# One inference step of a hybrid decoder: the first of seven products completed in PSUM, ScalarE's copies ahead of its roundings, the second weight sum on VectorE

## The reference

```python
def macaron_ffn(x, g_pre, w_gate, w_up, w_down, g_post):      # FFN_DIM = 4096
    n = rms_norm(x, g_pre)
    f = (jax.nn.silu(n @ w_gate) * (n @ w_up)) @ w_down
    return x + 0.5 * rms_norm(f, g_post)

h = macaron_ffn(x, ffn1...)      # stage one
h = token_mixing(h, ...)         # spatial gating and a causal depthwise convolution
h = cross_attend(h, ...)         # 4 heads over 256 memory tokens
h = macaron_ffn(h, ffn2...)      # stage two
```

## Time and profile before

| | before |
|---|---|
| time, median of 3 runs | 1690.36 us (1689.71 to 1690.53) |
| profiled execution, time / span | 1686.61 / 1684.7 us |
| TensorE matmul busy | 1580.3 us, 94% of the span |
| VectorE busy | 1321.5 us, 78% |
| ScalarE busy | 840.4 us, 50% |
| GpSimd busy | 425.3 us, 25% |
| mean granted TensorE clock | 0.994 |

### The profile page before, as it was taken

One profiled execution on the slowest core, in us unless ns is written; L12 is line 12 of the kernel. 1 busy time (PEld: TensorE's weight loads), 2 busy tenths in 40 slices (PEclk: granted clock), 3 DMA queues, 4 the chain that ended last, 5 costly groups with the idle time before them and its releaser, 6 DMA issues.

```text
span 1684.7 us, 28941 instructions
## 1 busy us (share of the span) xinstructions
PE 1580.3 (94%) x11628; PEld 1504.7 (89%) x11628; DVE 1321.5 (78%) x1715; ACT 840.4 (50%) x1496; POOL 425.3 (25%) x319
## 2 busy tenths in 40 slices
PE   8999999999999979999999999989999999999987
PEld 7998999999899969998989869889999998999987
DVE  5878888888888886999454533888888888888886
ACT  6455555554555555652453433555554545455444
POOL 2022433424243330000010100012334242433424
PEclk9999999999999989999999999999999999999998
DMA  5132223232222332233353543123232323223221
GB/s 172 51 101 89 87 76 100 76 101 76 91 86 76 101 118 67 76 101 114 101 177 110 194 146 101 35 72 96 78 99 75 101 76 97 79 78 99 76 76 57
DMA packets 121460, 159.12 MB, mean 94 GB/s; under 512 B 3645, under 2 KB 98449, under 8 KB 121320
## 3 DMA queue, kind: packets, MB, share of 16 engines
q1 hardware_dynamic: 115744, 138.16, 25.9%
q0 software_dynamic: 5488, 19.10, 3.3%
q10 hardware_dynamic: 96, 0.02, 0.0%
HBM read 152.22 MB, written 5.40 MB: 94 GB/s over the span
## 4 chain that ended last, share of the span: by engine, by line
PE 45%; DVE 36%; issue 10%; ACT 5%; POOL 2%; DMA 1%; DVEq 0%; SPq 0%; ACTq 0%; POOLq 0%
PE slot L2370 22%; PE slot L2169 15%; DVE mo L1548 5%; DVE wu L1646 4%; DVE f L1956 4%; DVE q L1637 4%; POOL raw L737 2%; DVE wu L1641 2%; PE slot L2215 2%; DVE wu L1656 2%; DVE turned L1552 1%; DVE wu L1651 1%; ACT wu L992 1%; DVE f L1758 1%; DVE wu L1661 1%
## 5 line engine op out<-in xcount | busy, mean ns | idle before, releaser
L2370 PE MATMUL slot<-nb,wu 128*128 128x288 f32 x4704 | 653.8, 297 | 58.2 <-ACT part L1046 25.4
L2370 PEld LDWEIGHTS slot<-nb,wu 128*128 128x128 f32 x4704 | 630.4, 188 | 77.9 <-ACT part L1046 34.8
L2370 PE MATMUL slot<-mo,wu 128*128 128x288 f32 x2688 | 373.1, 297 | 13.1 <-DVE mo L1548 3.8
L2370 PEld LDWEIGHTS slot<-mo,wu 128*128 128x128 f32 x2688 | 360.6, 188 | 23.0 <-issue 8.9
L737 POOL TENSOR_TENSOR raw<-raw,q 128x512 f32<-128x512 f32 x88 | 118.9, 1351 | 729.2 <-DVE q L1637 555.5
L1656 DVE TENSOR_TENSOR wu<-raw,wu 128x1024 fp32r<-128x1024 f32 x88 | 141.1, 1603 | 34.4 <-ACT wu L992 34.4
L742 POOL TENSOR_TENSOR raw<-raw 128x512 f32<-128x512 f32 x88 | 118.3, 1344 | 132.6 <-DVE wu L1651 132.6
L1646 DVE TENSOR_TENSOR wu<-q,wu 128x1024 fp32r<-128x1024 f32 x86 | 130.9, 1522 | 19.8 <-ACT wu L985 19.8
L1034 ACT ACTIVATE part<-slot 128x288 f32<-128x288 f32 (+1 forms) x84 | 41.3, 491 | 204.8 <-PE slot L2370 204.8
L2169 PE MATMUL slot<-mid,wp 128*128 128x288 f32 x960 | 133.0, 297 | 4.4 <-DVE mid L1480 2.3
L2169 PE MATMUL slot<-n,wp 128*128 128x288 f32 x960 | 134.8, 298 | 2.1 <-issue 1.7
(11 more groups left out here) (305 smaller groups left out, 2130.2 us busy)
## 6 DMA issues: line engine op xcount, KB each, us to landing
raw<-in_ffn_w_gate_dram SPq DMA_DIRECT2D x32, 1024.0 KB, 5.3
raw<-in_ffn_w_up_dram SPq DMA_DIRECT2D x32, 1024.0 KB, 5.4
raw<-in_ffn_w_down_dram SPq DMA_DIRECT2D x64, 512.0 KB, 4.3
raw<-in_mix_w_in_dram SPq DMA_DIRECT2D x8, 1024.0 KB, 5.5
kring<-in_cache_mem_k_dram POOLq DMA_DIRECT2D x6, 1024.0 KB, 5.2
raw<-in_xattn_w_k_dram SPq DMA_DIRECT2D x4, 1024.0 KB, 5.0
raw<-in_xattn_w_v_dram SPq DMA_DIRECT2D x4, 1024.0 KB, 5.0
raw<-in_mix_w_out_dram SPq DMA_DIRECT2D x4, 1024.0 KB, 5.0
```

The costliest lines, as they stand in the source:

```text
L2370: ins = pe.matmul(dst[:, q, 0:HALF], wu[:, p, wi, unit], x[:, xi], start=begins, stop=bool(ends), skip_group_check=not (start and 0 in pairs))
```

## The change

- **P1 completed in PSUM.** `copy_p1` copies x not to `part1` but to the y place, and P2 is added there. `take_c11` goes: in a gate group ScalarE takes its Silu straight from y (`silu_c11`), in an up group `multiply_c11` multiplies y by the gate. `take_y` adds y to f at once, `add_p1` on GpSimd goes, and `part1` with it.
- **`sum_q4` on VectorE** in place of GpSimd, behind take_c22 and its multiplication.
- **ScalarE's order.** copy_p7 and high_q13 come ahead of the roundings of 2 and 4; in a down group copy_p1(n+1) comes behind high_a2(n+1).
- **VectorE's order.** conv_low 756 right behind late_sum; take_c22 right behind low_q2; low_q13 ahead of conv_low 2 and 4; take_x ahead of low_a2; multiply_c21 ahead of low_a2; conv_low 3 and 1 behind early_sums.
- **Head.** low_a2, high_a2, copy_p1 of group 0 ahead of the second pair's sums and roundings.
- **End.** The operands 5, 6 and 7 of the last pair are summed and rounded one by one; the last group's P6 and P7 parts are added by VectorE straight from PSUM (`take_second`, `take_third`); its P3 comes ahead of P4; fewer rows are added on VectorE and more on TensorE (`ROW_SUMS`); memory_roots comes behind the root of stage one and memory_rows behind pre2's.

The diff, cut to its core (places, counts and renamed semaphores of the parts above are left out):

```diff
@@ GpSimd, ffn @@
-                def sum_q4(n): ...
-                def add_p1(n):
-                    pool.wait_ge(p1_copied, group_count(name, n))
-                    nc.gpsimd.tensor_tensor(f_part(n, 0, 1), f_part(n, 0, 1), part1[:, :, :], ALU.add).then_inc(f11_part, 1)
-                    if adds(n):
+                    if adds(n) and n + 1 < NG:
                         add_p6(n)
-                    if n + 1 < NG:
-                        sum_q4(n + 1)
-                    if adds(n):
+                    if adds(n) and n + 1 < NG:
                         subtract_p7(n)
-                    if adds(n + 1):
-                        add_p1(n + 1)
@@ ScalarE, ffn @@
                 def copy_p1(n):
+                    u = group_use(name, n, "y")
                     act.wait_ge(p1_done, group_count(name, n))
-                        dst = part_of(n, part1, 0)
-                    nc.scalar.activation(dst, x_of(n), ACT.Copy).then_inc(p1_copied, 1)
+                    act.wait_ge(slot_free[u % 4], u // 4)
+                    before = GATES_BEFORE[n]["y"]
+                    if before is not None:
+                        act.wait_ge(c21_silu, gated_count(name, pair_of(before)))
+                    nc.scalar.activation(y_of(n), x_of(n), ACT.Copy).then_inc(p1_copied, 1)
+                def silu_c11(n):
+                    ...
+                    act.wait_ge(p2_done, group_count(name, n))
+                    free(nc.scalar.activation(gate_c[:, 0, t1], y_of(n), ACT.Silu), group_use(name, n, "y"))
                 def silu_rest(n):
-                    nc.scalar.activation(gate_c[:, 0], gate_c[:, 0], ACT.Silu).then_inc(c11_silu, 1)
+                    nc.scalar.activation(gate_c[:, 0, t2], gate_c[:, 0, t2], ACT.Silu).then_inc(c12_silu, 1)
+                def last_up(n):
+                    conv_high("5", LAST_PAIR, (s75_sum, turned_count(name, LAST_PAIR)))
+                    conv_high("6", LAST_PAIR, (s6_sum, pair_count(name, LAST_PAIR)))
+                    act.wait_ge(job_done, group_jobs(name, n))
+                    high_q4(n + 1)
+                    copy_p1(n + 1)
+                    conv_high("2", LAST_PAIR, (c12_mul, gated_count(name, LAST_PAIR)))
+                    high_a11(n + 2)
@@ first_group @@
+                    high_a2(0)
+                    copy_p1(0)
                     conv_high("1", 1, made_plain(1, 1))
-                    copy_p1(0)
-                    conv_sums_of(1)
-                    high_a2(0)
-                    conv_high("4", 1, (s4_sum, pair_count(name, 1)))
                     high_a11(1)
                     high_q4(0)
+                    conv_sums_of(1)
@@ group @@
                     copy_p6(n)
+                    if n == LAST_UP + 1:
+                        conv_high("7", ...)
+                        conv_high("4", ...)
                     if is_kind(n - 1, "gate"):
                         silu_rest(n - 1)
-                            conv_sums(n - 1)
-                            conv_late(n - 1)
+                    if turn:
+                        conv_sums(n - 1)
                     if more:
                         high_q2(n + 1)
+                    if is_kind(n, "gate"):
+                        silu_c11(n)
                     copy_p7(n)
                     if more:
                         high_q13(n + 1)
-                        if n != LAST_UP:
+                        if n != LAST_UP and not is_kind(n, "down"):
                             copy_p1(n + 1)
+                    if turn:
+                        conv_late(n - 1)
                     if is_kind(n, "up"):
                         conv_early(n)
                     if more:
                         high_a2(n + 1)
+                        if is_kind(n, "down"):
+                            copy_p1(n + 1)
@@ VectorE, ffn @@
+                def sum_q4(n):
+                    s = group_slab(name, n)
+                    dve.wait_ge(q2_lo, group_count(name, n))
+                    V.tensor_tensor(a11_of(s), a12_of(s), a11_of(s), ALU.add).then_inc(q4_sum, 1)
-                def take_c11(n): ...
                 def multiply_c11(n):
-                    V.tensor_tensor(up_c[:, 0, t1], up_c[:, 0, t1], gate_c[:, 0, t1], ALU.mult).then_inc(c11_mul, 1)
+                    dve.wait_ge(*y_freed(name, n - 1))
+                    dve.wait_ge(p2_done, group_count(name, n))
+                    u = group_use(name, n, "y")
+                    free(V.tensor_tensor(up_c[:, 0, t1], slot(u)[:, 0, 0:HALF], gate_c[:, 0, t1], ALU.mult), u)
@@ group: the whole new order @@
                     if n == LAST_UP + 1:
                         for k in ("7", "4", "3"): conv_low(k, LAST_PAIR)
                     if n == 0:
                         sum_4(1); take_c22(0)
                     elif more:
                         sum_q13(n + 1)
                     if turn:
                         late_sum(n - 1); conv_low("756", pair_of(n - 1))
                     if adds(n): take_p5(n)
                     if down: take_y(n)
                     if up: multiply_c11(n)
                     if more: low_q2(n + 1)
                     if down and not adds(n): take_p5(n)
                     elif n and not down: take_c22(n)
                     if up: multiply_c22(n)
                     if more:
                         sum_q4(n + 1); low_q13(n + 1)
                     if turn:
                         conv_low("2", pair_of(n - 1)); conv_low("4", pair_of(n - 1))
                     if n == LAST_UP: conv_low("1", pair_of(n))
                     if up: multiply_c21(n)
                     if down: take_x(n)
                     if more and n != LAST_UP: low_a2(n + 1)
                     if up: early_sums(n)
                     if n == LAST_UP:
                         take_c12(n); multiply_c12(n); low_a2(n + 1); conv_low("2", LAST_PAIR)
                         sum_7(LAST_PAIR); sum_4(LAST_PAIR); low_a11(n + 2)
                     else:
                         if up:
                             for k in ("3", "1"): conv_low(k, pair_of(n))
                         if n + 2 < NG: low_a11(n + 2)
                         if down: take_z(n)
                         else: take_c12(n)
                     if more: low_q4(n + 1)
@@ last_group @@
                     take_p5(n)
+                    take_second(n)
                     take_y(n)
+                    take_third(n)
                     add_rows(slice(0, T), 2, 1, 0)
-                    if beside:
-                        beside()
-                    for i in (4, 6):
+                    for i in (4, 6) if not behind else ():
                         add_rows(t2, 5, i)
+                    take_z(n)
+                    for i in (5, 7) if not behind else ():
+                        add_rows(slice(0, 2 * P), 6, i)
                     take_x(n)
-                    for i in (5, 7):
-                        add_rows(t1, 6, i)
-                    take_z(n)
-                    for i in (5, 7):
-                        add_rows(t2, 7, i)
@@ TensorE @@
                 def p2(n):
-                    wait_place(n, "y")
+                    pe.wait_ge(p1_copied, count(n))
-                    product(n, P2, y_of(n), True, [p2_done])
+                    product(n, P2, y_of(n), False, [p2_done])
@@ last_groups @@
-                    group(d + 1)
+                    p6(d + 1)
+                    p2(d + 1)
+                    p7(d + 1)
+                    p3(d + 1, False)
+                    p4(d + 1, True)
@@ sum_rest @@
-                pe.wait_ge(f_added, 9 * (STAGE["ffn1"] + 1))
+                pe.wait_ge(f_added, rows_added("ffn1"))
                 fold_in(name, facc, True, True)
-                for i in (4, 6):
-                    for j in range(2):
+                for tiles, strips, count in (((4, 6), (2, 3), 5), ((5, 7), (0, 1), 6), ((4, 6), (0, 1), 7), ((5, 7), (2, 3), 8)):
+                    pe.wait_ge(f_squared, 8 * STAGE["ffn1"] + count)
+                    for i in tiles:
+                        for j in strips:
```

More of the change, by code:

```diff
@@ L757, in ffn @@
                 sum_q2(0)
-                sum_q4(0)
                 for n in range(NG):
@@ L1189, in ffn, with others @@
                 if name == "ffn1":
-                    root(post, D, "half", lambda: prepare(behind + 2))
+                    def others():
+                        prepare(behind + 2)
+                        beside()
+                    root(post, D, "half", others)
             act.wait_ge(eps_set, 3)
@@ L1774, in first_group @@
                     multiply(7, 1)
+                    low_a2(0)
+                    conv_low("1", 1)
+                    low_a11(1)
                     for e in range(2):
@@ L1778, in first_group @@
                     sum_6(1)
-                    conv_low("1", 1)
-                    low_a2(0)
-                    sum_4(1)
+                    sum_q13(1)
                     conv_low("756", 1)
-                    conv_low("4", 1)
```

(32 more changed lines are left out.)

227 lines of the change are left out of this document (124 added, 103 removed).

## The result

The changed kernel takes 1605.65 us (median of 4 runs, 1604.52 to 1609.32) against 1690.03 us (4 runs, 1687.41 to 1690.53): ratio 0.951, 95% interval 0.949 to 0.953. The prediction was 1607 us, range 1594 to 1640. The profiled execution took 1606.58 us, span 1604.8, which is 79.9 less than before.

The account below looks back on a forecast made before the run. TensorE, busy 94%, was taken as the bound, its waits as the pool. Loop gains of 68.4 us, plus 4.6 + 5.2 + 4.7 + 3.5 - 3, made 83.4: 1690.4 - 83.4 = 1607 us, range 1594 to 1640.

Parts of the forecast that it names:

- Copies ahead of roundings: Turns: copy_p7 and take_c22 ahead of the roundings of 2 and 4 cut TensorE's waits, 16.2 + 12.0 us a stage.
- sum_q4 on VectorE: Every group: 88 sums add 53 us of VectorE queue, take_c11 gives back 20; worth the up groups' waits, 12 us.
- VectorE's dates: Loop: VectorE's results stay in time; low_q13 in down groups tightest, 0.3 us to spare; 3 us allowed in all.
- P1 in PSUM: Loop: copy_p1 writes the y bank and P2 adds to it; no new wait but P2's, cost nothing.
- Heads: Group 0 of each stage: P2 and P4 start earlier; 2.3 us a stage, 4.6 in all.
- Last groups: Last 19 products of a stage: operands one by one remove waits before P5 and P2; 2.6 us a stage, 5.2.
- Between the stages: From stage one's last product to the root: root at E + 2.7, 4.7 us less; clock perhaps 1 more, left out.
- Tail: After the last product: sums of rows begin at E + 2.0; gain 0.3 to 6 us, 3.5 taken.
- a new wait that takes part back: Rival for the loop: tight dates missed by 0.5 us in 88 groups, 44 us lost, 1651 us; chance 0.21.
- VectorE as the bound: Rival for the loop: sum_q4 lands in each group's chain and blocks stay, slower than before, 1723 us; chance 0.05.

Follow-up runs that it names:

- the first experiment: Kernel before with only the turns' order changed: roundings of 2 and 4 behind copy_p7 and high_q13 on ScalarE, take_c22 and low_q13 on VectorE; 1673.34 us.
- the 24 extra GpSimd sums: Changed kernel plus one GpSimd sum of 576 elements behind subtract_p7 in down groups that add, its result unused; 1619.23 us, ratio 0.9596.
- the two together: Kernel before with the turns' new order and sum_q4 on VectorE, P1 still completed through SBUF; 1643.99 us, ratio 0.9737.
- the one with the gains moved: Changed kernel with the four output gains of stage two on ScalarE instead of GpSimd; 1604.11 us, ratio 0.9499.

## Why the prediction held, point by point

The state that I described came: a span of 68.1 us, TensorE waiting in the turns for copy_p7, 0.20 us each, sum_q4 at 0.7 us in 74 of 88 places (1.8 in 14 down groups, one block as foreseen), the root 3.1 us behind the last product. The total was right to 1.4 us, and that closely by luck: against the forecast the loop gave 4.8 us more (70.2 in the trace, 65.4) and the pass 1.2 more, heads, last groups and tail 2.3, 1.3 and 2.9 less. What was wrong is whose gain it is.

1. *Copies ahead of roundings*, priced at 16.2 + 12.0 a stage, 56 us: wrong as a term of its own. Of the 56, 20 are the waits for copy_p7 (1.26 + 0.26 - 0.4, 14 times; 0.47 + 0.26 - 0.4, 12 times), and ScalarE's order did measure 16 and 18 of them with P1 in PSUM (1622 to 1605, 1624 to 1606). The turn that is left is as told too: 0.20 of wait and 0.26 of refill, against my 0.4. The other 36 are mostly take_c22, 0.93 and a refill 26 times, 31 us. That wait does go with VectorE's order, but it goes with sum_q4's move as well, so it is no gain of the order alone. And in the kernel before, with nothing else changed, GpSimd's sums make take_x late in the next down group (six waits, 8.1 us in stage one). There both engines' order together measured 16 us (1690 to 1673), and 13 with sum_q4 moved (1657 to 1644).
2. *sum_q4 on VectorE*, priced at 12 us: 33 us in the kernel before (38 in its loop), 29 with the order there, and nothing in the company of the rest. It was mis-sized both ways, because it isn't a term of its own: it, the order and add_p1 each remove some of the same blocks.
3. *VectorE's dates*: held in all but the last groups. low_q13 in the down groups is the tightest, 0.1 us to spare in one of them where I had 0.3; in the two last groups it costs 0.32 us.
4. *P1 in PSUM*, "cost nothing": right. The copy of 288 elements into PSUM takes 0.399 us, the one into SBUF took 0.403 (L1021 before). The step that failed is that I priced only its cost. With VectorE's new order, and heads and ends, it is worth 68 us alone (1690 to 1622), 51.8 of them in the loop; behind order and sum_q4 it still adds 21 there (48.9 to 70.2). How this divides was not tried. Part of the 52 must be VectorE's order, which alone takes away the wait for take_c22, as in the first experiment. add_p1's blocks, with the other parts in, may be some 14 us; that is an estimate from the 24 extra GpSimd sums, which did not all stand where the 28 of add_p1 had stood. 56 take_c11 gone from the queue may be worth some more (52 us of VectorE work cost 22). The share of P1 in PSUM against that of VectorE's order stays open.
5. *Heads*: 2.3 of 4.6 us. P7's date was right (8.2 us after P1's start; 81.6 - 73.5 = 8.1 foreseen). P4's was not: I left out that GpSimd's sum_q2 and low_q4 block each other (1.97 and 1.78 us), with sum_4, the rounding of 4 and copy_p7 in the queue behind.
6. *Last groups*: 3.9 of 5.2 (the dates that I named add up to 33.65 us, not 33.8; 34.6 was measured). The dates named were those that waited (conv_low 7, copy_p7, low_q13), and take_second was a fourth.
7. *Between the stages*: 5.9 against 4.7. The root came 3.1 us after the last product's end (2.7 foreseen), and the clock stayed at its upper level (1.00 in all windows from 582 to 591, 0.50 in the earlier trace rows), about the 1 us that I had left out.
8. *Tail*: 0.6 against 3.5. VectorE's four sums of squares took 3.46 us beside GpSimd's gains, so the sums of rows began at E + 3.5, not E + 2.0, and the clock fell while they ran (0.59 in 1584 to 1588). They were done at E + 8.9, my date for the fallen clock, by two errors that cancel: 1.5 us late in starting, 5.3 us long in place of 6.8. I took 3.5 as a middle between a fallen clock and one that stays up; it fell. Even the 0.6 is not clear of chance: with the tail of before the span ended 23.8 to 25.3 us after the last product in four traces.

Of the rivals, a new wait that takes part back is what the order alone and the two together do in the kernel before; with P1 in PSUM and VectorE's new order it is gone. VectorE as the bound is near: 0.6 us more a group cost 0.25 a group.

The exclusive lock of the Trainium skill (SBUF — State Buffer, Who interferes with whom) is borne out by the rows above: sum_4 takes 1.44 us in place of 0.45 and ends 0.3 us behind GpSimd's sum, which itself takes 1.38 us, hardly more than its free 1.30. One is held back, the other is not, so they don't share speed. The Trainium skill warns that work moved between GpSimd and VectorE might not help (Perfetto Trace Analysis, Optimizing Scalar/DVE Operations). So it was in the changed kernel (0.9508 against 0.9507); in the kernel before the same move gained 33 us.

## What to carry to other kernels

Where two engines lock one another out, count their work together in each group, not by engine: a helper that is busy for 15 to 25% can hold the chain. One wait may go by any of several edits, and then its gain comes once, as that for take_c22 did. So terms of a sum that share a cause can't be priced one by one from the waits of the kernel before; ask of each wait which other part of the change would also remove it. And price what a removed instruction gives back, not only what its replacement costs.

## What the runs showed of the hardware

- Under mutual blocks both engines' rows are stretched: GpSimd's sum of 576 elements shows 1.43 us or 2.42, VectorE's rounding of 1024 elements 1.21 or 2.46. The extra is the other's instruction: in the rows of the order alone the two queues, both full, alternate one by one.
- A ScalarE copy from PSUM into PSUM costs what one into SBUF does: 0.399 and 0.643 us for 288 and 576 elements, against 0.403 and 0.646 for the same copy before (L1021).
- The first group of stage one starts anywhere between 73.39 and 75.64 us in kernels with the same code ahead of it, as much as the small gains sought here; the distance from P1(0) to the last product's end was the better measure (506.19 and 507.15 us in the two stages of the changed kernel, 506.17 and 507.14 in the one with the gains moved).
